# Two second-gate projections moved from the merge stage into the last mixer iteration, by way of a scratch tensor

## What is computed

```python
h = _rmsnorm(x, norm_pre[l])
proj = jnp.einsum('bsd,dn->bsn', h, w_in[l])
qa, ka, va, za, qb, kb, vb, ob, zb, igb, fgb, ga, gb = _split(proj, sizes)
oa = _diff_attention(qa, ka, va, lam)
ya = oa.reshape(B, S, W_A) * jax.nn.silu(za)
hb = _mlstm(qb_c, kb_c, vb, ig, fg)
hb = jax.nn.sigmoid(ob.astype(jnp.float32)).reshape(B, S, H_B, HEAD_DIM_B) * hb
yb = hb.reshape(B, S, W_B) * jax.nn.silu(zb)
merged = (jax.nn.sigmoid(ga) * jnp.einsum('bsw,wd->bsd', ya, w_a[l])
          + jax.nn.sigmoid(gb) * jnp.einsum('bsw,wd->bsd', yb, w_b[l]))
out = jnp.einsum('bsd,de->bse', merged, w_out[l])
x = x + _rmsnorm(out, norm_post[l])
```

## Time and profile before

| | |
|---|---|
| three runs | 2123.1, 2126.87, 2127.84 us; median 2126.87 us |
| profiled execution | span 2120.4 us from first to last instruction; only the span is given for it, and the median of the runs lies 6.5 us above |
| PE | 2001.6 us busy, 94% of the span |
| DVE, ACT, POOL | 60%, 40%, 6% |
| DMA | 200.27 MB, 94 GB/s on average |
| costliest groups near the change | L1691 to L1693, mixer jobs: 576 matmuls each; L2377 to L2379, merge jobs: 384 each |

### The profile page before, as it was taken

How to read it: one execution, slowest core, us unless ns; L and a number is a source line. 1 busy time by engine, 2 the same in 40 slices (tenths; PEclk the granted TensorE clock), 3 DMA queues, 4 the chain that set the end, 5 groups by cost and what they waited for, 6 DMA issues and landing times. The chain is left out here.

```text
span 2120.4 us, 29425 instructions
## 1 busy us (share of the span) xinstructions
PE 2001.6 (94%) x11256; PEld 1610.3 (76%) x11256; DVE 1271.7 (60%) x2415; ACT 855.6 (40%) x1376; POOL 136.8 (6%) x114
## 2 busy tenths in 40 slices
PE   5989999999999999969998999999998999999998
PEld 2667878888887878757776877777776678888877
DVE  7776878796869687659445545345353345733543
ACT  5644353544445353169213243434443337700221
POOL 0020202111120202000000000000000000000000
PEclk8999999999999999989999999999999999999999
DMA  7222323232324233458113211211212116211242
GB/s 282 82 75 69 105 72 103 68 96 75 109 64 118 69 106 108 132 187 280 46 44 125 75 60 40 70 61 50 90 30 80 60 62 227 80 50 50 80 119 80
DMA packets 128971, 200.27 MB, mean 94 GB/s; under 512 B 56596, under 2 KB 88084, under 8 KB 127808
## 3 DMA queue, kind: packets, MB, share of 16 engines
q1 hardware_dynamic: 128832, 198.39, 29.4%
HBM read 156.22 MB, written 42.11 MB: 94 GB/s over the span
## 5 line engine op out<-in xcount | busy, mean ns | idle before, releaser
L795 PE MATMUL p_job<-h_hi,w_hi 128*128 128x512 f32 x768 | 322.0, 419 | 18.0 <-DVE h_lo L185 16.5
L797 PE MATMUL p_job<-h_hi,w_lo 128*128 128x512 f32 x768 | 302.4, 394 | 0.0
L796 PE MATMUL p_job<-h_lo,w_hi 128*128 128x512 f32 x768 | 302.2, 393 | 0.0
L1691 PE MATMUL m_job<-h_hi,m_hi 128*128 128x512 f32 x576 | 251.2, 436 | 5.0 <-issue 4.2
L1693 PE MATMUL m_job<-h_hi,m_lo 128*128 128x512 f32 x576 | 229.3, 398 | 0.0
L1692 PE MATMUL m_job<-h_lo,m_hi 128*128 128x512 f32 x576 | 227.8, 396 | 0.0
L795 PEld LDWEIGHTS p_job<-h_hi,w_hi 128*128 128x128 f32 x768 | 145.6, 190 | 59.8 <-issue 16.4
L796 PEld LDWEIGHTS p_job<-h_lo,w_hi 128*128 128x128 f32 x768 | 146.0, 190 | 35.1 <-issue 7.9
L797 PEld LDWEIGHTS p_job<-h_hi,w_lo 128*128 128x128 f32 x768 | 145.8, 190 | 31.4
L1691 PEld LDWEIGHTS m_job<-h_hi,m_hi 128*128 128x128 f32 x576 | 109.8, 191 | 50.6 <-issue 31.2
L633 ACT ACTIVATE pre<-p_job 128x512 f32<-128x512 f32 x96 | 56.8, 592 | 178.3 <-PE p_job L797 176.7
(11 more groups left out here) (395 smaller groups left out, 4164.5 us busy)
## 6 DMA issues: line engine op xcount, KB each, us to landing
w_raw<-in_w SPq DMA_DIRECT2D x49, 512.0 KB
m_raw<-in_w SPq DMA_DIRECT2D x49, 512.0 KB, 3.7
rows<-grows SPq DMA_DIRECT2D x32, 512.0 KB, 6.5
ada<-in_ada_w SPq DMA_DIRECT2D x8, 1024.0 KB, 5.3
z_scr<-pre SPq DMA_DIRECT2D x16, 512.0 KB, 2.6
o_scr<-oT SPq DMA_DIRECT2D x64, 128.0 KB, 1.8
ob<-o_scr SPq DMA_DIRECT2D x16, 512.0 KB, 4.8
zb<-z_scr SPq DMA_DIRECT2D x16, 512.0 KB, 4.6
```

The costliest lines, as they stand in the source:

```text
L795: nc.tensor.matmul(bank, hi, h_hi[:, k, cut], start=(k == 0), stop=False)
L796: nc.tensor.matmul(bank, hi, h_lo[:, k, cut], start=False, stop=False)
L797: last = nc.tensor.matmul(bank, lo, h_hi[:, k, cut], start=False, stop=(k == KD - 1))
L1691: nc.tensor.matmul(bank, hi, h_hi[:, k, cut], start=(k == 0), stop=False)
```

## The change

The blocks gb 6 and gb 7 are no longer projected in the merge. They become the seventh and eighth gate job of the mixer's last iteration, are stored in `g_scr` as they come out of PSUM, and in the merge SP loads each into `sgb`, where ACT takes the sigmoid in place. `MERGE_JOBS` has 22 jobs, and ends with ab 4, ab 5, ab 6, ab 7 without a gate job between them. The banks of the last jobs and of the output tiles are exchanged, and four of the low parts of the merged blocks are made one job later in DVE's loop. The number of matmuls stays the same. Beside what is shown, the third weight list gets the columns of gb 6 and 7, and `g_scr` two rows more.

```diff
 GATE_ORDER = [("zb", 0), ("zb", 1), ("zb", 2), ("zb", 3), ("ob", 0), ("ob", 1),
-              ("za", 0), ("za", 1), ("za", 2), ("za", 3), ("ob", 2), ("ob", 3)]
-GATE_SHARE = (0, 2, 2, 2, 6)
+              ("za", 0), ("za", 1), ("za", 2), ("za", 3), ("ob", 2), ("ob", 3), ("gb", KD - 2), ("gb", KD - 1)]
+GATE_SHARE = (0, 2, 2, 2, 8)
...
 MERGE_JOBS = ([("ga", c) for c in range(KD)] + [("gb", 0)]
-              + [job for c in range(1, KD) for job in (("gb", c), ("ab", c - 1))] + [("ab", KD - 1)])
+              + [job for c in range(1, KD - 2) for job in (("gb", c), ("ab", c - 1))]
+              + [("ab", c) for c in range(KD - 3, KD)])
...
-        OUT, RES = (6, 2), (0, 4)
+        OUT, RES = (2, 6), (0, 4)
...
-            return (4, 6) if c < KD - 1 else (0, 4)
+            return (0, 2) if c == KD - 2 else (4, 6)
...
-        LAST_GATE = at[("gb", KD - 1)]
+        LAST_GATE = at[("gb", KD - 3)]
...
+            for c in range(KD - 2, KD):
+                sp.wait_ge(m3, c)
+                sp.dma_start(sgb[:], io["g_scr"][gate_row("gb", c)]).then_inc(in_s, 16)
...
-            for c in range(KD):
-                if 0 < c < KD - 1:
-                    act.wait_ge(m3, c)
-                if c == KD - 1:
+            for c in range(KD - 2):
+                if c == KD - 3:
                     act.wait_ge(job_done, LAST_GATE + 1)
-                    for k in range(KD - 2):
+                    for k in range(KD - 4):
                         merged_hi(k)
+                if c:
                     act.wait_ge(m3, c)
                 gate(at[("gb", c)], sgb)
+            merged_hi(KD - 4)
+            for c in range(KD - 2, KD):
+                act.wait_ge(in_s, 16 * (c - KD + 3))
+                for i in range(2):
+                    cut = slice(i * HALF, (i + 1) * HALF)
+                    nc.scalar.activation(sgb[:, cut], sgb[:, cut], ACT.Sigmoid).then_inc(sg_done, 1)
+                if c == KD - 2:
+                    merged_hi(c - 1)
             nc.scalar.preload_act_table_set(EXP_LN)
             merged_hi(KD - 2)
...
+                    elif c == KD - 2:
+                        pe.wait_ge(sg_done, 2 * (2 * KD - 2))
                     elif c == KD - 1:
-                        pe.wait_ge(sg_done, 4 * KD - 2)
+                        pe.wait_ge(m2, c - 1)
                     else:
                         pe.wait_ge(m2, c)
                     for q in range(2):
-                        if c == KD - 1 and q == 1:
-                            pe.wait_ge(m1, c)
...
                 if J + 2 < NJ:
                     split(J + 2)
                 what, c = MERGE_JOBS[J]
-                if J == LAST_GATE:
-                    for k in range(KD - 2):
+                if J == LAST_GATE + 1:
+                    for k in range(KD - 4):
                         merged_lo(k)
                 if what == "ab":
+                    if c >= KD - 3:
+                        merged_lo(c - 1)
                     if c == KD - 1:
-                        merged_lo(KD - 2)
                         for k in range(HA):
                             wo_low(k)
                     dve.wait_ge(job_done, J + 1)
```

More of the change, by code:

```diff
@@ L1479, with gate_row @@
 GATE_ORDER = [("zb", 0), ("zb", 1), ("zb", 2), ("zb", 3), ("ob", 0), ("ob", 1),
-              ("za", 0), ("za", 1), ("za", 2), ("za", 3), ("ob", 2), ("ob", 3)]
-GATE_SHARE = (0, 2, 2, 2, 6)
+              ("za", 0), ("za", 1), ("za", 2), ("za", 3), ("ob", 2), ("ob", 3), ("gb", KD - 2), ("gb", KD - 1)]
+GATE_SHARE = (0, 2, 2, 2, 8)
+def gate_row(name, c):
+    return 3 * c + MIX_GATES.index(name) if name in MIX_GATES else 3 * HB + c - (KD - 2)
 def mix_jobs():
@@ L1553, in send @@
                         behind += [(1 + 2 * q, ("tap", j, q)) for q in range(TAPS)] + [(10, ("silu", j))]
-                    if name in MIX_GATES:
+                    if name in MIX_GATES or name == "gb":
                         out.append(("gstore", s[1]))
@@ L1733, in sync @@
                         sp.wait_ge(evac_done, 2 * s[1] + 2)
-                        sp.dma_start(io["g_scr"][3 * head + MIX_GATES.index(name)], gt[:]).then_inc(g_store, 16)
+                        sp.dma_start(io["g_scr"][gate_row(name, head)], gt[:]).then_inc(g_store, 16)
                     elif s[0] == "store":
@@ L1739, in sync @@
                         sp.dma_start(io["a_scr"][HA + g], hT[:]).then_inc(a_stored, 16)
-            sp.wait_ge(g_store, 16 * 3 * HB)
+            sp.wait_ge(g_store, 16 * len(GATE_ORDER))
             sp.wait_ge(a_stored, 32 * HB)
@@ L2192, in stage_merge @@
         p_ss = banks[6:8]
-        OUT, RES = (6, 2), (0, 4)
+        OUT, RES = (2, 6), (0, 4)
         def ab_banks(c):
-            return (4, 6) if c < KD - 1 else (0, 4)
-        cst = sem("e_cst"); nys = sem("e_nys"); in_a = [sem("e_ina0"), sem("e_ina1")]; in_g = [sem(f"e_ing{m}") for m in range(NY)]
+            return (0, 2) if c == KD - 2 else (4, 6)
+        cst = sem("e_cst"); nys = sem("e_nys"); in_a = [sem("e_ina0"), sem("e_ina1")]; in_g = [sem(f"e_ing{m}") for m in range(NY)]; in_s = sem("e_ins")
         ob_done = sem("e_ob"); sq_done = sem("e_sq"); ss_done = sem("e_ss"); ln_done = sem("e_ln"); ri_done = sem("e_ri")
@@ L2424, in residual @@
                 else:
-                    pe.wait_ge(m1 if t == 0 else m2, KD)
+                    pe.wait_ge(m1, KD - 1 + t)
                 for k in range(KD):
@@ L2437, in tensor @@
                 else:
-                    pe.wait_ge(sg_done, 4 * KD)
+                    pe.wait_ge(m2, KD)
                 for k in range(KD):
@@ L2687, in _layout @@
     gates2 = 4 * wa + 5 * wb
+    gate0 = gates2 + 2 * HB
     at2 = {"qa": 0, "ka": wa, "va": 2 * wa, "za": 3 * wa, "qb": 4 * wa, "kb": 4 * wa + wb, "vb": 4 * wa + 2 * wb,
-           "ob": 4 * wa + 3 * wb, "zb": 4 * wa + 4 * wb}
+           "ob": 4 * wa + 3 * wb, "zb": 4 * wa + 4 * wb, "gb": gate0 + D}
     second = [[(0, gates2 + HB, HB), (32, gates2, HB)]]
@@ L2692, in _layout @@
     win2, cqk = a["w_in_2"][0], a["conv_qk_2"][0]
-    gate0 = gates2 + 2 * HB
     ga = _tiles(win2, [[(0, gate0 + c * P, P)] for c in range(KD)])
@@ L2759 @@
     "mrows": (2 * HB, T),
-    "g_scr": (3 * HB, P, T),
+    "g_scr": (3 * HB + 2, P, T),
     "a_scr": (HA + HB, P, T),
```

## The result

The changed kernel takes 2143.2 us (median of 4 runs, 2137.3 to 2149.9) beside 2126.9 us for the kernel before (4 runs): a ratio of 1.0082, 95% interval 1.0060 to 1.0103. A second comparison on another occasion gave 2146.7 against 2122.5 us, 1.0112 (1.0099 to 1.0125). It is slower, by 16 to 24 us, where 21.4 had been forecast; the predicted median of 2148.3 is 5.1 us above the first result and 1.6 above the second. The runs of one kernel spread by more than that: of the four in the first comparison the shortest, 2137.3 us, had a mean granted clock of 0.981 and the longest, 2149.9, one of 0.976.

The account below looks back on a forecast made before the run. PE was taken as the bound, busy 94% of the span. The terms -21.8, +24.95, +11.0 and +7.3 gave +21.4 us: span 2141.8, median 2148.3 us, 1.0% slower, range 2138 to 2155.

Parts of the forecast that it names:

- Out of the merge, -21.8: Merge: two jobs of 10.88 us each leave it and give their full price, -21.8 us.
- The mixer, +24.95: Last mixer iteration: 32 more slices, +22.4 us, and losses to gaps and clock of 16.8 instead of 14.25, +2.55.
- the 0.9 at the first `turn`: Last mixer iteration: with no slow stretch behind the start, PE comes 0.9 us too early to the first `turn`.
- 1.7 us behind each of four gaps: Last mixer iteration: each of four gaps of 1.5 to 2.3 us costs 1.7 us more of clock, together 6.8.
- the rival that short gaps cost no clock: Last mixer iteration: the four gaps stay but cost no clock, 6.8 us less: +14.6, 2141.5 us; chance 0.24.
- Ab 4 to ab 5, +11.0: Merge: PE waits 9.3 us for DVE to empty ab 4's banks, then loses 1.7 us to the low clock.
- The end, +7.3: End of the merge: late loads of gb 6 and 7 delay the last sigmoid and the chain to output tile 0, +7.3 us.
- The forecast's bounds, 3.3 and 12: End of the merge: delay of 3.3 us if the loads were free, 12 if each load took twice as long.
- 258: Merge: predicted window in us from the first merge matmul to the last ab job, of 268.47.
- the 6.5 us that the forecast adds: Whole kernel: the median of the runs lies 6.5 us above the profiled span, taking 2141.8 to 2148.3.

Follow-up runs that it names:

- merge_fixed: low_banks with gb 6 and 7 loaded early into two empty buffers, and two output weight loads and that of `norm_post` later: 2121.8 us, 0.9994 of before.
- low_parts: The changed kernel with the four low parts moved back one job earlier, beside ab 4: 2141.9 us, 1.0084 of the kernel before.
- low_banks: low_parts with ab 5 on banks 0, 1, 4, 5 and other banks for ab 6 and 7: 2131.7 us, 1.0049 of the kernel before.
- mixer_alone: The kernel before with the two gate jobs added to the last mixer iteration, stored but never read, merge unchanged: 2148.1 us, 1.0110 of before.
- rows_swapped: The changed kernel with the two new scratch rows for gb 6 and gb 7 exchanged: 2143.9 us in one run.
- merge_alone: The changed kernel with six gate jobs in the mixer, gb 6 and 7 read from other scratch rows, their projections left out: 2121.2 us, 0.9985 of before.
- all_four: merge_fixed with the last mixer iteration's weight loads issued ahead of the stores: 2115.5 us, 0.9969 of the kernel before.
- all_early: all_four with the weight loads issued ahead of the stores in mixer iterations 1 to 4: 2114.1 us, 0.9949 of the kernel before.
- before_early: The kernel before with the last mixer iteration's weight loads issued ahead of the stores, nothing else: 2116.3 us, 0.9957 of before.
- before_early_all: The kernel before with weight loads issued ahead of the stores in mixer iterations 1 to 4: 2117.9 us, 0.9965 of before.

## Why the prediction was right, and where its terms were off

The mechanism held in the merge: two waits, in the places named and for the reasons given. In the mixer the gaps came where they were forecast, three of the four for the reason given; the fourth and the price of all four were not as told.

- **Out of the merge, -21.8.** The two jobs are gone. In merge_fixed, with the waits repaired, the merge is 247.78 us long for 268.47: 20.7 less, with 0.8 left in the wait at L2391.
- **The mixer, +24.95.** The traces give +22.2 and +19.6 (142.40 and 139.85 against 120.21). In length the gaps are as forecast: 1.13, 2.17, 2.06, 1.69 and 2.44 us at the start and at blocks 1, 3, 6 and 7, for 1.0, 2.2, 2.3, 1.5 and 2.1; the 0.9 at the first `turn` was 0.2; 9.9 in all for 10.0. What was oversized is the clock: I took 1.7 us behind each of four gaps. Only two had a slow stretch, worth 4.50 x 0.37 = 1.7 and 4.35 x 0.34 = 1.5 us: 3.1 for 6.8. The second trace had one, 1.7 for 6.8. Seven traces have these four gaps (the changed kernel's two, low_parts, low_banks, merge_fixed, mixer_alone, rows_swapped), and 8 of their 28 gaps were followed by a slow stretch. So the rival that short gaps cost no clock was nearer than the forecast. It pairs badly with length, since 2.06 was followed by 1.00 once and by 0.61 once, in the same place of the same kernel. For block 7 the length was right by luck: the forecast has the blend stand behind a load for most of 7.4 us, and the load had landed when DVE came to the split. The load was issued at 1751.61, and the shortest landing of such a load is 3.5 us, so by this estimate it came at 1755.1 or later, and `sm`, which the split also follows, began at 1755.98. The two nearly tie, and an earlier load gained nothing.
- **Ab 4 to ab 5, +11.0.** The wait is 9.31 by window for 9.3. The slow stretch was too small at 1.7: ab 5 took 13.56 us for 10.88, 2.7 more (1.9 in the second trace). Low_banks shows the whole term, 11.1 us in the traces; low_parts shows which part of the wait was the low parts'.
- **The end, +7.3.** From the end of ab 7 (2034.77) to the end is 113.2 us, before 106.1: +7.1, with 5.72 idle ahead of tile 0 for "about 6". Behind that tile 0 runs at 0.50 for 4.3 us, 2.2 lost, which the forecast does not name; but its last slices had to wait for DVE before (1.7 us at L2446) and hardly do now, so most of it costs nothing. The forecast's bounds, 3.3 and 12, change one of the two loads only; with both free or both doubled its own working gives about 0 and 15.3. The two loads landed in a median of 3.6 us in merge_alone and 3.7 in the changed kernel, for 4.0. Merge_fixed takes them off the chain, and with them 9.9 us, more than the term: the traces have 6.5 us less ahead of tile 0 and 4.2 behind its start, where the slow stretch and the waits for the residual loads go as well.
- **Missed.** The 2.09 us ahead of L2387 and the 1.7 behind it (4.38 x 0.38), so that the last ab job ended 262.7 us after the first merge matmul and not 258. In the second trace the wait is 1.18 us and no slow stretch follows, 1.2 for 3.8. The forecast puts the two new stores beside PE's work, at no cost. The merge's first loads stand behind the last stores in SP's queue, and the last of these, that of `hT`, lands later. All ten traces with eight gate jobs have this wait, of 0.7 to 2.1 us, and none of the four with six has it; that it comes from the late landing was not tested by itself. The changed kernel and merge_alone, two instructions of SP each:

```profile
1772.79 0.79 SPq L1744 DMA_DIRECT2D a_scr<-hT  x1
...
1779.01 0.33 SPq L2241 DMA_DIRECT2D ny<-in_norm_y  x1
```

```profile
1748.86 0.79 SPq L1744 DMA_DIRECT2D a_scr<-hT  x1
1753.29 0.33 SPq L2241 DMA_DIRECT2D ny<-in_norm_y  x1
```

SP stands 6.2 us for the stores instead of 4.4, and these are the times from issue to landing of the `hT` store itself.

The errors nearly cancel, which is luck: of the traces' +27.6 us, 4.1 lie ahead of the change; -2.8 in the mixer, +1.0 behind ab 4, -0.2 at the end and +3.8 missed turn +21.4 into +23.2, against 23.5 left. In the second trace, +21.7 with 4.1 ahead, it is -5.3 in the mixer and +1.2 at L2387, and 17.6 are left. The medians, +16.3 and +24.2, lie to both sides of it; the range, 2138 to 2155, held both. There is luck in the last step too. Of the 6.5 us that the forecast adds to come from the span to the median, 1.7 to 1.9 are the difference that every single run has between its time and its span; the rest is that before's profiled execution was a short one. The changed kernel's was a long one, with a span 6.2 us above the forecast's 2141.8, while its median lies 5.1 below the forecast.

The figure of the Trainium skill's page "DMA: Bandwidth & Descriptors" (section "Anatomy of one DMA — SWDGE (gpsimd) path"), 3.2 us for 512 KB, would have given a sum 5.5 us lower by the forecast's estimate. It is stated for transfers that GpSimd issues, and SP issues these. The first median lies just there, but not for that reason: the loads of `m_raw` took a median of 4.0 us and those of `sgb` 3.7 in the changed kernel, so the rows were the better guide to the loads.

## What to carry to other kernels

Before filling idle time of the bounding engine with work from elsewhere, ask who made the gap. Here two of the four were made by a prefetch that stood in its queue behind a store that waited for a third engine: moving the load ahead of the store gave 0.43%, while the work moved in found as many gaps made anew by its own loads and splits, and won next to nothing. Where two waits end at nearly the same time, as at block 7, taking one away gains nothing. And when a job that separated two users of the same accumulators is moved away, look at what the draining engine does between them; other banks, with four instructions placed a job earlier, gave back 11 us without changing any work.

## What was not expected of the hardware

- After gaps of nearly the same length, in the same place of the same program, the clock did different things. Ahead of `turn` of block 3 the changed kernel stood 2.06 us in both traces: 1.00 followed in the first, 0.61 in the second. The gap of 2.2 to 2.4 us at block 7 was followed by 0.62 to 0.66 in three traces (the changed kernel's first, all_four, all_early) and by 1.00 in seven. Before's gap of 1.83 had 0.61 behind it, and in merge_alone, whose mixer is the same, one of 1.74 had 1.00. From the last mixer iteration on, each of the 17 waits of 3.56 to 9.14 us in all traces was followed by 0.50 to 0.62 over 4.4 us. What decides it after the shorter ones stays open.
- The loss behind a wait did not follow its length: a wait of 4.60 us led to 0.50 for 4.4 us and 0.91 for the 4.2 behind, waits of 9.14 us to 0.50 and 0.87 in one trace and to 0.56 and 1.00 in another.
- SP stands between its store of `hT` and the merge's first load for 4.4 us in all four kernels with six gate jobs in the last iteration (before, merge_alone, before_early, before_early_all), and for 6.0 to 6.5 us in all ten with eight, whatever else was changed. It is the landing of that store, 4.4 us against 6.0 to 6.4. The last `g_scr` store ahead of it took 4.6 us instead of 2.7 in the changed kernel, but 3.3 in mixer_alone, where `hT` still took 6.1. It isn't the row that the `g_scr` store writes (rows_swapped). The cause was not found.
